# Four token phases in place of two for a depthwise convolution on TensorE, with strided writes to PSUM

## What is computed

```python
u = rms_norm(h, g_mix);  z = u @ w_in                    # [value | gate | pool | gate A | gate B]
gates = sigmoid(z[..., c3:] + b_gate)
a = a_val * sigmoid(a_gate)                              # conv branch
a = depthwise_conv(a, w_dw, width=31, centred) + b_dw
y_conv = silu(layer_norm(a, ln_g, ln_b)) @ w_conv_out
m = window_mean(p, windows 2, 4, 8, 16 by channel group) - p    # pooling branch
y_pool = (m @ w_pool * pool_scale) @ w_pool_out
h = h + (gates_A * y_conv + gates_B * y_pool) @ w_o
v = rms_norm(h, g_ffn)
h = h + (silu(v @ w_ffn_gate) * (v @ w_ffn_up)) @ w_ffn_down
out = rms_norm(h, g_final)
```

## Time and profile before

| | |
|---|---|
| median of 3 runs | 989.99 us (989.78 to 990.99) |
| profiled execution, its own time | 991.0 us |
| span of its slowest core (core 0) | 989.5 us (cores 985.5 to 989.5) |
| TensorE busy | 962.3 us, 97% |
| VectorE, ScalarE, GpSimd busy | 433.1, 291.7, 154.9 us |
| mean granted TensorE clock | 0.997 of full speed |

### The profile page before, as it was taken

The page is one execution under the profiler, slowest core; times in us unless marked ns, Lnnn a source line. Parts: engine busy times, 40 slices in busy tenths (PEclk is TensorE's granted clock), DMA queues, the critical chain, the costliest instruction groups (busy, mean ns, idle before and its releaser), DMA issues.

```text
span 989.5 us, 14699 instructions; the slowest of 8 cores (985.5 to 989.5 us)
## 1 busy us (share of the span) xinstructions
PE 962.3 (97%) x5176; PEld 474.0 (48%) x5176; DVE 433.1 (44%) x632; ACT 291.7 (29%) x486; POOL 154.9 (16%) x216
## 2 busy tenths in 40 slices
PE   3999999999899999999999999999999999999996
PEld 2755555554344444444444444444444444444485
DVE  4776689653885323233476212211112211342454
ACT  3853143356952121110544111111111111121121
POOL 3002221124740000001771110110000000000000
PEclk9999999999999999999999999999999999999999
DMA  9705988775773111226965444553222005122222
GB/s 212 233 4 98 217 215 177 231 171 119 132 170 62 22 20 24 32 32 155 356 165 133 74 82 90 101 98 47 34 31 43 12 1 181 75 85 85 85 86 85
DMA packets 41158, 105.81 MB, mean 107 GB/s; under 512 B 5760, under 2 KB 14208, under 8 KB 38400
## 3 DMA queue, kind: packets, MB, share of 16 engines
q0 software_dynamic: 21472, 51.06, 28.7%
q1 hardware_dynamic: 19616, 53.82, 16.3%
HBM read 115.80 MB, written 21.04 MB: 138 GB/s over the span
## 4 chain that ended last, share of the span: by engine, by line
PE 95%; DMA 2%; DVE 1%; POOL 1%; issue 1%; ACT 0%; DVEq 0%; ACTq 0%; POOLq 0%
PE ps L370 92%; PE ps L664 3%; DMA xb<-xp 1%; DMA wslot<-w_pool_out 1%; DVE uT L397 0%; POOL d L384 0%; DVE h2b L397 0%; POOL wslot L199 0%; ACT sqx L381 0%; DVE sqx L384 0%; ACT ps L381 0%; ACT sq L381 0%; DVE h2b L384 0%; DVEq L1033 0%; DVEq L193 0%
## 5 line engine op out<-in xcount | busy, mean ns | idle before, releaser
L370 PE MATMUL ps<-vT,wslot 128*128 128x512 bf16 x1408 | 304.4, 379 | 0.0
L370 PE MATMUL ps<-uT,wslot 128*128 128x416 bf16 (+3 forms) x1536 | 292.3, 349 | 3.1 <-DVE uT L397 2.3
L370 PEld LDWEIGHTS ps<-uT,wslot 128*128 128x128 bf16 x1536 | 151.1, 99 | 140.8 <-issue 12.6
L370 PEld LDWEIGHTS ps<-vT,wslot 128*128 128x128 bf16 x1408 | 137.7, 98 | 167.1 <-issue 1.6
L384 DVE TENSOR_TENSOR fT<-ps,sgf 128x512 bf16<-128x512 f32 x88 | 60.7, 691 | 228.8 <-PE ps L370 228.8
L370 PE MATMUL ps<-fT,wfd 128*128 128x512 bf16 (+1 forms) x880 | 153.2, 336 | 0.0
L381 ACT ACTIVATE sgf<-ps 128x512 f32<-128x512 f32 x88 | 52.5, 597 | 241.5 <-PE ps L370 234.2
L370 PEld LDWEIGHTS ps<-fT,wfd 128*128 128x128 bf16 x880 | 86.1, 98 | 67.8 <-issue 1.7
L370 PE MATMUL ps<-cell,wslot 128*128 128x512 bf16 x512 | 114.8, 379 | 0.0
L397 DVE SCALAR_TENSOR_TENSOR zt<-zt,ps 128x512 f32<-128x512 f32 x64 | 43.9, 687 | 106.1 <-PE ps L370 106.0
L381 ACT ACTIVATE zt<-ps,hb 128x512 f32<-128x512 f32 x64 | 43.9, 691 | 138.1 <-PE ps L370 138.1
(11 more groups left out here) (76 smaller groups left out, 610.6 us busy)
## 6 DMA issues: line engine op xcount, KB each, us to landing
rep<-ad SPq DMA_DIRECT2D x128, 129.5 KB, 4.7
wslot<-w_in POOLq DMA_DIRECT2D x40, 256.0 KB, 7.0
h1d<-h1b SPq DMA_DIRECT2D x4, 2048.0 KB, 10.1
h2b<-h1d SPq DMA_DIRECT2D x4, 2048.0 KB, 13.7
h1b<-xr SPq DMA_DIRECT2D x3, 2048.0 KB, 19.6
out<-h2b SPq DMA_DIRECT2D x3, 2048.0 KB, 8.1
wslot<-w_ffn_gate POOLq DMA_DIRECT2D x22, 256.0 KB, 5.3
wslot<-w_ffn_up POOLq DMA_DIRECT2D x22, 256.0 KB, 5.2
```

Source lines behind the costliest of these rows:

```text
L370: S.op(PE, lambda e: e.matmul(out, lhsT=lhsT, rhs=rhs, start=start, stop=stop), [lhsT, rhs], [out], signal=stop if signal is None else signal)
```

## The change

Tokens are kept in four phases (`PH` = 4). A `rep` tile is now 8 channels x 4 phases x 4 shifts, so a matmul contracts 16 neighbouring tokens, and its 32 output columns are 8 channels x 4 output phases. Three matmuls cover the 31 taps plus 3 (the third starts one column after the second and uses only its last shift). One bank holds 32 channels x 2048 tokens. 384 convolution matmuls are issued in place of 512, all over 512 columns. The convolution weights grow from 512 to 768 columns a group.

`im2col` issues as many DMAs as before, each over 128 partitions with 32 outer rows and runs of 517 elements (1034 bytes) in place of 64 partitions and 1036 elements (2072 bytes). `a_out` writes runs of 312 and 208 elements in place of 624 and 416. The layer norm has one statistic over all tokens in place of two halves: two fp32 mask matmuls in place of four, two short VectorE additions ahead of them, and no copies of mean and 1/std to PSUM. `silu` is four ScalarE instructions of 256 columns and four DMAs of 512-byte runs per half and chunk, in place of two of 512 columns and two of 1024-byte runs.

Tiles of later stages now hold 512 neighbouring tokens. `pool_tile`, the gate tiles `A` and `Bm`, and `C` read their moving operand phase by phase and write PSUM through `alt`, so neighbouring columns of the matmul land four fp32 elements apart in the bank. `P` and `w_o` write contiguously, `w_o` in four runs of 128.

```diff
-HALO = 15
+HALO = 16
+PH = 4
...
-HE = EXT // 2
+HE = EXT // PH
...
-RW = TOK // 2 + 12
+RW = TT + 5
...
-    mT = at("mT", [128, KC, 2, TOK // 2], BF16, oM)
+    mT = at("mT", [128, KC, TOK], BF16, oM)
...
-    cell = [at(f"cell{c}", [128, 2, 2, 2, TT], BF16, oB + c * EXT * 4) for c in range(KC)]
-    actX = [[cell[g // 2][:, g % 2, h, 0, :] for h in range(2)] for g in range(NG)]
-    actT = [[cell[c][:, b % 2, b // 2, 1, :] for b in range(NB)] for c in range(KC)]
+    dcell = [at(f"d{c}", [128, 2, 4, 256], F32, oB + c * EXT * 4) for c in range(KC)]
+    cell = [at(f"cell{c}", [128, 2, 4, 2, 256], BF16, oB + c * EXT * 4) for c in range(KC)]
+    actT = [[cell[c][:, b // 2, :, 1, 128 * (b % 2):128 * (b % 2) + 128] for b in range(NB)] for c in range(KC)]
...
     def par(ap):
-        return ap.rearrange("p (e x) -> p e x", e=2)
+        return ap.rearrange("p (e x) -> p e x", e=PH)
 
     def alt(ap):
-        return ap.rearrange("p (x e) -> p e x", e=2)
+        return ap.rearrange("p (x e) -> p e x", e=PH)
...
         for k in range(KC):
-            mm(par(b[:, 0:n]), w(f"pool{c}", k), uT[:, k, :, o // 2:(o + n) // 2], k == 0, k == KC - 1)
-        act(alt(psb[c][:, o:o + n]), par(b[:, 0:n]), AF.Copy)
+            mm(alt(b[:, 0:n]), w(f"pool{c}", k), uT[:, k, :, o // PH:(o + n) // PH], k == 0, k == KC - 1)
+        act(psb[c][:, o:o + n], b[:, 0:n], AF.Copy)
...
-            for j in range(4):
-                for r in range(2):
-                    src = bass.AP(a_d, (128 * c + 64 * i + 16 * j) * EXT + HE * r, [[EXT, 16], [1, 4], [1, RW]])
-                    S.dma(SP, rep_sem[r_i], rep[r_i][r::2, j, 0:RW], src, val=tot)
+            for j in range(8):
+                src = bass.AP(a_d, (128 * c + 64 * i + 8 * j) * EXT, [[HE, 32], [1, 4], [1, RW]])
+                S.dma(SP, rep_sem[r_i], rep[r_i][:, j, 0:RW], src, val=tot)
...
-            for h in range(2):
+            for i in range(2):
                 ps = nb()
-                for q in range(4):
+                for q, x0 in enumerate((0, 4, 5)):
                     for j in range(4):
                         o = ps[32 * j:32 * j + 32, :]
-                        lt = cw[g % 4][:, j, q, :]
-                        x0 = h * TT + 4 * q
-                        r_ = rep[rix(g)][:, j, x0:x0 + TT]
+                        lt = cw[g % 4][:, i, q, j, :]
+                        r_ = rep[rix(g)][:, 4 * i + j, x0:x0 + TT]
...
-    def tile_mm(wname, rhs, weff_c=None):
+    def tile_mm(wname, rhs, weff_c=None, out=None):
...
-            mm(b[:], lhsT, rhs(k), k == 0, k == KC - 1)
+            mm((out or alt)(b[:]), lhsT, rhs(k), k == 0, k == KC - 1)
...
     def u_rhs(b):
-        x0 = (HALO + b % 2) // 2 + (b // 2) * TT
-        return lambda k: uT[:, k, 1 - b % 2, x0:x0 + TT]
+        x0 = HALO // PH + 128 * b
+        return lambda k: uT[:, k, :, x0:x0 + 128]
...
-        ps = tile_mm(None, lambda k: mT[:, k, b % 2, (b // 2) * TT:(b // 2 + 1) * TT], weff_c=c)
+        ps = tile_mm(None, lambda k: mT[:, k, TT * b:TT * b + TT], weff_c=c, out=lambda a: a)
...
+    def ln_stat():
+        pm, pq = psum[6], psum[7]
+        for acc, ps in ((acc_s, pm), (acc_q, pq)):
+            tt(DVE, acc[:, :, 0, :], acc[:, :, 0, :], acc[:, :, 1, :], ALU.add)
+            mm(two(ps[:]), pmask[:], acc[:, :, 0, :], True, True)
...
     def silu(h, c):
-        for g in (2 * c, 2 * c + 1):
-            act(actX[g][h], dpart(g, h), AF.Silu, bias=pc[:, PC_LNB + g:PC_LNB + g + 1],
-                scale=pc[:, PC_LNG + g:PC_LNG + g + 1])
-        for g in (2 * c, 2 * c + 1):
-            r0 = 64 * (g % 2)
-            S.dma(SP, rg_sem[h * KC + c], cell[c][r0:r0 + 64, :, h, 1, :], actX[g][h], val=32)
+        for q in range(4):
+            G = 4 * c + q
+            act(cell[c][:, h, q, 0, :], dcell[c][:, h, q, :], AF.Silu, bias=pcc(PC_LNB, G), scale=pcc(PC_LNG, G))
+        for q in range(4):
+            S.dma(SP, rg_sem[h * KC + c], cell[c][32 * q:32 * q + 32, h, :, 1, :], cell[c][:, h, q, 0, :], val=64)
...
             for k in range(KC):
-                mm(ps[:], w(f"wo{c}", k), mrg[k][b], k == 0, k == KC - 1)
+                mm(par(ps[:]), w(f"wo{c}", k), mrg[k][b], k == 0, k == KC - 1)
```

More of the change, by code:

```diff
@@ L294, in build_nc @@
     z = oZ
[L295 to L298, removed]
+    RB = 16 * HE
+    rep = [at(f"rep{i}", [128, 8, HE], BF16, o) for i, o in
+           enumerate((z, z + RB, oB + 6 * EXT * 4, oB + 7 * EXT * 4, z + 24064, z + 32384))]
+    z += 2 * RB
+    dsq = [at("dsq0", [128, 2, 2, 256], F32, z), at("dsq1", [128, 2, 2, 256], F32, oW + 8192)]
     z += 4096
@@ L301, in build_nc @@
     z += 2 * PW * 4
-    aT = [at(f"aT{i}", [128, 2, HE], BF16, z + i * EXT * 2) for i in range(2)]
+    aT = [at(f"aT{i}", [128, PH, HE], BF16, z + i * EXT * 2) for i in range(2)]
     z += 2 * EXT * 2
@@ L558, in windows @@
         src = psb[c][:, lo:lo + width]
-        m = mT[:, c, :, t0 // 2:(t0 + n) // 2]
-        own = alt(psb[c][:, HALO + t0:HALO + t0 + n])
+        m = mT[:, c, t0:t0 + n]
+        own = psb[c][:, HALO + t0:HALO + t0 + n]
         if wd == 2:
-            out.append(lambda: (tt(DVE, m, alt(src[:, 0:n]), own, ALU.subtract),
+            out.append(lambda: (tt(DVE, m, src[:, 0:n], own, ALU.subtract),
                                 win_done.add(c) if ti else None))
@@ L800, in step @@
             if g not in far:
[L801 to L804 removed]
+                tt(DVE, d, d, half2(psum[6], h), ALU.subtract)
+            tt(DVE, d, d, half2(psum[7], h), ALU.mult)
+            if h and g == NG - 1:
+                zfree.append(ln_ids[1])
             if g >= 4 and g % 2 == 0:
@@ L838, in build_nc @@
     Bm(0, 2)
-    for h in range(2):
-        ln_stat(h)
+    ln_stat()
     Bm(0, 3)
     release("gB0")
-    for h in range(2):
-        ln_rstd(h)
+    ln_rstd()
     bg.extend(ln_steps(0))
@@ L1078, in _host_inputs @@
     for col, v in ((PC_BDW, arr("b_dw")), (PC_LNG, arr("ln_g")), (PC_LNB, arr("ln_b"))):
-        pc[:, col:col + NG] = np.repeat(v.reshape(NG, 64), 2, 1).T
-    zero = np.zeros((1, D), f32)
-    wdw = arr("w_dw")
-    taps = np.stack([np.concatenate([wdw, zero], 0), np.concatenate([zero, wdw], 0)], 0)
-    vals = taps.reshape(2, 4, 8, NG, 4, 16).transpose(3, 5, 2, 4, 1, 0)
-    cw = np.zeros((NG, 16, 8, 4, 4, 16, 2), f32)
-    for i in range(16):
-        cw[:, i, :, :, :, i, :] = vals[:, i]
+        pc[:, col:col + 2 * NG] = np.repeat(v.reshape(2 * NG, 32), PH, 1).T
+    wdw = arr("w_dw").reshape(KW, NG, 2, 4, 8)
+    cw = np.zeros((NG, 8, PH, 4, 2, 3, 4, 8, PH), f32)
+    for q in range(3):
+        for a in range(4):
+            if q == 2 and a < 3:
+                continue
+            for pi in range(PH):
+                for po in range(PH):
+                    tap = PH * (4 * q + a if q < 2 else 8) + pi - 1 - po
+                    if 0 <= tap < KW:
+                        for ch in range(8):
+                            cw[:, ch, pi, a, :, q, :, ch, po] = wdw[tap, :, :, :, ch]
     pmask = np.zeros((128, 128), f32)
-    pmask[0::2, 0::2] = 1.0 / D
-    pmask[1::2, 1::2] = 1.0 / D
+    for e in range(PH):
+        pmask[e::PH, e::PH] = 1.0 / D
     T = SEQ + NMETA
@@ L1135, in _gather @@
 def _gather(results, core):
-    o = np.asarray(results[core]["out"]).reshape(2, 2, 128, KC, TT)
-    return o.transpose(0, 4, 1, 3, 2).reshape(TOK, D)
+    o = np.asarray(results[core]["out"]).reshape(NB, 128, KC, TT)
+    return o.transpose(0, 3, 2, 1).reshape(TOK, D)
 _NC_CACHE = {}
```

117 lines of the change are left out of this document (54 added, 63 removed).

## The result

| | before | changed |
|---|---|---|
| median, beside one another | 990.49 us (989.78 to 991.81) | 1246.2 us (1241.57 to 1248.63) |
| ratio, 95% interval | | 1.2574 (1.2543 to 1.2605), slower |
| profiled execution, slowest core | span 989.5 | span 1239.7 |
| TensorE busy, and the rest of the span | 962.3, 27.2 | 1182.3, 57.4 |

The account below looks back on a forecast made before the run. TensorE, busy 962.3 of 989.5 us, was taken as the bound. Removed matmuls saved 8.8 us, less 0.7, 1.2, 1.5 and 1.0 of added costs: 4.4 us less, forecast 985.5 us, range 981.5 to 988 (chance 0.62).

Parts of the forecast that it names:

- (h): 1152 pooling input, gate and `C` matmuls writing PSUM four elements apart: taken as nothing, upper bound 236 us.
- The rival: Strided PSUM writes double every `pool_tile`, gate and `C` matmul: 236 us more, 1217 us; chance 0.19.
- (a): Convolution: 128 of 512 matmuls removed, 7.1 us saved.
- (b): Layer norm: two of four fp32 mask matmuls removed, 1.7 us saved.
- (c): Two short VectorE additions ahead of the mask matmuls: 0.7 us taken, between 0 and 1.3.
- (d): 64 silus of 256 columns for 32 of 512: later `weff` write, TensorE waits 1.2 us, 0 to 2.5.
- (e): 64 gathers with 512-byte runs for 32 with 1024-byte runs: 1.5 us taken, 0 to 6.6.
- (f): Shifted copies with twice the runs: free in mid-stage, 1.0 us taken for the last chunk, 0 to 1.9.
- (g): Larger tap weights and shorter `ad` writes lie under the same slack; four-run moving operands cost nothing.
- waits take the gain: Rival: added VectorE work, silus, gathers and copies at upper ends, 12.3 against 8.8 us, 993.5 at worst; chance 0.10.

Follow-up runs that it names:

- g16: The changed kernel with the recorder's dependency granule at 16 bytes in place of 32; 1217.0 us, 1.2268.
- nat_light: `nat_whole` with the tap weights' third part loaded only for its 32 non-zero partitions; 1.0013.
- contig_g16: `contig` with the dependency granule at 16 bytes in place of 32; 1010.9 us, 1.0172.
- whole_ad: `contig_g16` with `aT` written to DRAM once a chunk in runs of 4160 bytes, in place of two writes; 1.0060.
- nat_split: `nat_whole` with the change's two writes of `aT` a chunk, in runs of 624 and 416 bytes; 1.0189.
- nat_whole: `whole_ad` with the permutation moved to ScalarE's and VectorE's reads of PSUM, so all SBUF accesses are contiguous; 1.0078.
- light_taps: `contig_g16` with the third tap matrix loaded only for its 32 non-zero partitions; 1.0117.
- light_whole: `contig_g16` with both the edit of `light_taps` and that of `whole_ad`; 1.0055.
- mvRuns: Group of matmuls in `patterns` that reads and writes in four runs of 128; 14.0 us, against 13.9 contiguous.
- contig: The changed kernel with every matmul writing PSUM contiguously by phase and ScalarE restoring the order of the pooling input; 1062.6 us, 1.0729.
- patterns: No part of the block: groups of 64 matmuls differing in access pattern, and ScalarE and VectorE copies; matmuls 27.4 us interleaved, 13.9 contiguous.

## Why the prediction was wrong

The step that failed is (h), "I take nothing, by the nearest row, the two-run writes". It measured +228.2 us with what the false waits add, +219.6 in `g16` without them, against 236 at the upper bound. A write in two runs of 208 or more columns is not near to a write without neighbours at all: in the first all columns but one at the seam have their neighbour. The row that could have priced (h) did not exist in the trace, and I chose between ends 236 us apart by a row that shared only the word "strided". The rival had mechanism, place and size; its argument "no slow matmul anywhere in the trace" was empty, as no such write was there. The Trainium skill, "PSUM — Partial Sum Buffer", section Specifications, which I had weighed and set aside, has lines of 8 bytes and a slower matmul for writes that are not contiguous. The runs agree for elements that stand alone, and give that a size: twofold (27.4 against 13.9 us). They differ from its "any": pairs, which fill such a line, and runs of 128 are not contiguous as a whole either and were free (13.7 and 14.0 us), and there the measurement decides.

That the median of `g16`, 1217.0, equals the rival's 1217 is chance in part: its strided matmuls cost 219.6 and not 236 us, and TensorE waits 41.4 us in it, 14.2 more than before, where the rival took waits as hidden. The changed kernel itself is 29 us above the rival.

The other steps, in their order:

- (a) right in kind, 6.4 of 7.1 us: the convolution is busy 28.9 us before and 22.5 in `nat_light`. In the changed kernel itself it is 26.1: behind a wait of 4.23 us, for instance, 24 of its matmuls took 2.75 us in place of 1.49, and the granted clock there, 250 to 280 us, is 0.94.
- (b) right: one pair of mask matmuls, and the next tile begins 1.75 us behind the first of the two that stay (355.30 to 357.05), so a pair is worth the 1.7 us taken, as far as one pair tells of the other.
- (c) right in size: 0.8 us in `contig_g16` (`acc_s`), none in the changed kernel and in `nat_light`.
- (d) right in kind: silus of 256 columns take 597 ns (forecast "near 600"). TensorE waits 1.0 us for `weff` in the changed kernel (forecast 1.2), but there the slow gate tiles leave ScalarE more time; without the strided writes it is 1.4 to 2.5, mostly near the upper end.
- (e) its gathers by themselves 1.0022, some 2 us, where the whole step had 1.5, with the wait at 312 us and not at the first tile that reads them; no wait for the gathers in the changed kernel.
- (f) right where it looked: short runs alone cost 0, and in `nat_light` the last convolution waits 1.15 us for `rep`, for 1.0 taken. Wrong in "In the middle of the stage this is free": chunk 6, like the last, has one stage and not two between its copies and their use, and there `contig_g16` waits 10.3 us and `g16` 11.4.
- (g) wrong: "lie under the same slack". The shorter writes of `ad` cost 11 us (`contig_g16` to `whole_ad`), 11 (`nat_split` to `nat_whole`) and 6 (`light_taps` to `light_whole`), the taps 6 in one pair and nothing that is shown in two others. They take the same 16 DMA engines as the copies, busy 94% by the two queues of `contig_g16` above, so they are better priced as one load than as separate terms. Only the moving operands in four runs did cost nothing (`mvRuns`). Without (h) the forecast would still have missed: `contig_g16` is at 1.0172 (from 1.0106) and `nat_split` at 1.0189, some 1007 and 1009 us, where "waits take the gain" ended at 993.5 us.
- Not foreseen: the granule. 30 us in the changed kernel, 55 in `contig`. The section on the change gives a run length of 312 elements, 624 bytes, and the kernel's text the granule of 32 bytes; their quotient, 19.5, is not whole.

## What to carry to other kernels

Cost a new access pattern of TensorE by its innermost step, apart from how many runs it has: a step that leaves no two neighbours together doubled the matmul in PSUM, so let the matmul write runs or pairs and let ScalarE or VectorE permute as they read PSUM. Where a tracker of dependencies works in granules, divide every new row and piece length by the granule first, since a false wait looks in the trace like any other. Transfers in one stretch share the DMA engines: when several edits each load them a little, price the stretch as one load, and distrust that each fits under the same slack. Count the stages between a transfer and its use for every chunk, since at the end of a pipeline more than the last one can be short of them.

## What the hardware showed beyond that

In `patterns`, ScalarE and VectorE with 512 fp32 (mean ns is the last figure before the second bar):

```profile
L306 ACT ACTIVATE raOutstr<-ps 128x512 f32<-128x512 f32 x8 | 8.6, 1080 | 0.6
L316 DVE TENSOR_TENSOR dvOutstr<-ps,dsrc 128x512 f32<-128x512 f32 x8 | 8.5, 1066 | 0.7
L316 DVE TENSOR_TENSOR dvSbinstr<-dsrc 128x512 f32<-128x512 f32 x8 | 8.5, 1060 | 1.1 <-DVE dvSbinstr L316 0.5
```

A 16-byte step in SBUF, written or read, costs 1.5 to 1.8 times the contiguous 597 ns (ScalarE) and 692 ns (VectorE). The same step as a read of PSUM costs nothing: 603 and 690 ns. So a step that doubles TensorE's write to PSUM is free for these engines' reads of it. In the block, `psb` of 448 columns took 543 ns in `nat_light`, by strided reads of PSUM, 544 in the changed kernel without, and 985 in `contig`, written with a step.
